# Key numbers of the chosen pairs in a PEER router: an exclusive-or with ranked numbers and a minimum in place of compare, multiply and add

## The chip, the cores and the metric

The kernel runs on one core of one Trainium2 chip. The metric is the device time of one execution in microseconds (us), lower is better. The engines named below are PE (matrix products; PEld is its weight load), DVE (the vector engine), ACT (the scalar engine), POOL (GpSimd, which here mostly issues row gathers) and SP (whose queue issues the large weight loads).

## The reference, cut to what matters

One layer of a hybrid backbone over 640 tokens (128 context tokens, 512 latent ones), that is five tiles of 128 tokens. After the attention half of the layer comes PEER, an expert retrieval. Per token and head, a query is scored against two sets of 128 keys, the best 16 of each side are kept, the 16 by 16 sums are ranked again, and the best 16 pairs name the experts:

```python
s_half, i_half = lax.top_k(s, PEER_TOPK)
cand = s_half[:, :, 0, :, None] + s_half[:, :, 1, None, :]
cand_idx = i_half[:, :, 0, :, None] * N_KEYS + i_half[:, :, 1, None, :]
top_s, top_pos = lax.top_k(cand.reshape(t, PEER_HEADS, PEER_TOPK * PEER_TOPK), PEER_TOPK)
experts = jnp.take_along_axis(cand_idx.reshape(...), top_pos, axis=-1)
gates = jax.nn.softmax(top_s, axis=-1)
# per token: y = sum over its 128 experts of gate * gelu(u[expert] . x) * v[expert]
```

There are 8 heads, so 128 experts for each token.

## The kernel before, in words

**Tiles.** Tile 0 is the context; tiles 1 to 4 are the latent tokens. The router takes the tiles in the order 0, 1, 3, 4, 2. Tiles 0, 1 and 2 are "gathered": POOL fetches, for each of the 128 experts of a token, one row of `expert_u` for 128 tokens at once (128 rows of 4 KB) into one of eight slots, DVE multiplies and sums it with the tokens (one "dot", line 1341), and the slot is free again for POOL. Rows of `expert_v` are gathered likewise and added with weights (line 1585). Tiles 3 and 4 are "dense": PE multiplies them with all 16384 experts, streamed by SP as 128 blocks of 512 KB from `expert_uT` (line 795) and later 128 blocks of `expert_v` (line 858).

**The router.** `rank_keys` (lines 1527 to 1534) finds the best 16 keys of four half-heads at a time, `route(e, part)` has six parts: part 0 builds the candidate sums and the key numbers as floats (line 1426, a cast of 128x256) and finds the best eight, parts 1 and 2 find the places and the next eight, part 3 splits a place into two digits (lines 1444 to 1452) and looks up the first side's key numbers, part 4 looks up the second side's, part 5 makes expert numbers and gates. The look-up is `key_numbers(side)`, lines 1416, 1418 and 1420: compare each of the 128 digits with 0 to 15 (a cube of 8x16x16 = 2048 columns), multiply by the 16 key numbers, and add over the last axis. Each pass waits for the one before it.

**Order on DVE.** Everything on DVE is in program order. The stages: attention of the context; the merge and norm of tile 0; `choose(0)`, which is `rank_keys` and `route` of tile 0; four groups of eight dots of tile 0; `convolve(1)` (lines 1285 to 1300), for which ACT waits; three more groups; attention of the latent tokens with dots between its units; merges and norms of tiles 1 to 4 with value rows of tile 0 between them; `choose(1)` with value rows between its pieces; then `rank_keys` and `route` of tiles 3, 4 and 2, with a group of eight dots of tile 1 after most pieces (after the pieces named in `DOTS_AFTER`: parts 1, 3 and 5 of each tile's route among them); ten groups of dots of tile 2; then `gates()`, 32 steps of building one-hot rows (line 1627) and products with the gates, which wait in their turn for PE's last block of `expert_uT`; the rest of the dots; and the late values. PE's placement of gates (line 845) follows DVE's one-hot rows, and its stream over `expert_v` (line 858) follows the last product.

**Order on POOL.** POOL's gathers of tile 0 wait for the end of route(0) (line 596 and on), those of tile 1 for the end of route(1) and for all value rows of tile 0. POOL fetches in fours: after four dots have freed four slots it copies four row numbers (line 518) and issues four gathers (line 523).

Of the kernel before, what the change touches and what calls it, by code (L numbers as in the profile page):

```python
# [19 lines left out]
ALU = mybir.AluOpType  # L20
ACT = mybir.ActivationFunctionType
AX = mybir.AxisListType.X
F32 = mybir.dt.float32
U32 = mybir.dt.uint32

P = 128
# [13 lines left out]
PEER_HEADS, TOPK, NKEYS = 8, 16, 128  # L40
HK = PEER_HEADS * TOPK
CAND = TOPK * TOPK
KEPT = CAND // 2
GROUP = 8
GROUPS = HK // GROUP
SCALE = HD ** -0.5
# [98 lines left out]
def backbone(nc, x_prompt, x_sample, xT, ck_T, cache_v, c_T, w_ada, b_ada, w_in, convw_T, w_branch,  # L145
# [10 lines left out]
    with ExitStack() as ctx:  # L156
        def sem(name):
            return ctx.enter_context(nc.semaphore(name))
# [52 lines left out]
        EQ = [at({0: 14336, 1: 28672}.get(e, 45056), PEER_HEADS, CAND) for e in range(TILES)]  # L211
        LATE = {e: at(o, 4, HALF) for e, o in ((1, 26624), (3, 35840), (4, 37888), (2, 39936))}

        VR = [UR] + [[at(26624 + 1024 * i, D) for i in range(GROUP)]] * (TILES - 1)
        U2B = [at(47104, D), at(44032, D), at(47104, D)]
# [8 lines left out]
        def keep(*shape):  # L224
            v = at(small[0], *shape)
            small[0] += int(np.prod(shape))
            return v
# [3 lines left out]
        IDXS = keep(2 * PEER_HEADS * TOPK).bitcast(U32)  # L231
# [3 lines left out]
        IDXF = keep(2 * PEER_HEADS * TOPK)  # L235
# [7 lines left out]
        MODT, CONVW, MASK, IOTA = keep(16, 2), keep(4, 3), keep(3, COL_BAND), keep(NKEYS)  # L243
        CT2, SIL, SEL = keep(KD, 2), keep(KD, 2), keep(2)
        NMAX, RSUM, RINV = keep(3, 4), keep(3, 4), keep(3, 4)
        STAT, MV, RSTD = keep(12), keep(2), keep(2)
        SMAX, TOPS, GSUM = keep(HK), keep(PEER_HEADS, TOPK), keep(PEER_HEADS)
        POS, PA, AF, BF = SW[:, 0, :].bitcast(U32), SW[:, 1, :].bitcast(U32), SW[:, 2, :], SW[:, 3, :]
        assert small[0] <= 53184, small[0]

# [66 lines left out]
        dgelu_out, spread_done, spread_out = sem("dgelu_out"), sem("spread_done"), sem("spread_out")  # L317
        hot_i, hot_j = sem("hot_i"), sem("hot_j")
        gated, placed = sem("gated"), sem("placed")
        product = sem("product")  # L320
        zero_set, rank_done, rank_out = sem("zero_set"), sem("rank_done"), sem("rank_out")
        cols_ready, summed = sem("cols_ready"), sem("summed")

# [909 lines left out]
        def _(dve):  # L1233
# [66 lines left out]
                dve.tensor_tensor(Cy[:, :, own], Cy[:, :, own], ct, ALU.mult).then_inc(conv_step, 1)  # L1300

            dve.wait_ge(consts_in, 48)
            convolve(0)
            for g in range(5, 8):
                add_mods(g)
# [62 lines left out]
            def route(e, part):  # L1368

                base = PICKED[e] - PICKS_OF[e]  # L1370
                val = VAL.rearrange("p (h s k) -> p h s k", s=2, k=TOPK)
                idxf = IDXF.rearrange("p (h s k) -> p h s k", s=2, k=TOPK)
                cube = [P, PEER_HEADS, TOPK, TOPK]
                if part == 0:
                    dve.wait_ge(topk_step, 80 * (TURN[e] + 1))
                if part == 0 and e == 1:
                    dve.wait_ge(store_out[1], 48)
                if part == PARTS - 1 and e == 2:
                    dve.wait_ge(rank_done, 1)
                if part == 3 and e == 1:  # L1380
                    dve.wait_ge(store_out[0], 64)
                    dve.wait_ge(ut_done, TILES)
                if part == 3 and e == 3:
                    dve.wait_ge(ss_done, 4 * TILES)
                if part or e:
                    dve.wait_ge(pick_step, base + ROUTE_AT[part])
                step = [base + ROUTE_AT[part]]

                def done(ins):
                    step[0] += 1  # L1390
                    ins.then_inc(pick_step, 1)

                def settle():
                    dve.wait_ge(pick_step, step[0])

                cands = CANDS[e][:, :, 0:KEPT].rearrange("p h (a b) -> p h a b", b=TOPK)
                eq = EQ[e].rearrange("p h (a b) -> p h a b", b=TOPK)
                pos = POS.rearrange("p (h k) -> p h k", k=TOPK)
                smax = SMAX.rearrange("p (h k) -> p h k", k=TOPK)
                iota = IOTA[:, 0:TOPK].unsqueeze(1).unsqueeze(1).to_broadcast(cube)  # L1400
                digits = DIGITS[e] if e in DENSE else (AF, BF)
                gate = DGATE[e] if e in DENSE else GATE[e % 2]

                def best(lo):

                    for h in range(PEER_HEADS):
                        done(dve.max(TOPS[:, h, lo:lo + 8], CANDS[e][:, h, 0:KEPT]))

                def places(lo):
                    for h in range(PEER_HEADS):  # L1410
                        done(dve.max_index(pos[:, h, lo:lo + 8], TOPS[:, h, lo:lo + 8], CANDS[e][:, h, 0:KEPT]))

                def key_numbers(side):

                    digit = digits[side].rearrange("p (h k) -> p h k", k=TOPK)
                    done(dve.tensor_tensor(eq, digit.unsqueeze(3).to_broadcast(cube), iota, ALU.is_equal))
                    settle()
                    done(dve.tensor_tensor(eq, eq, idxf[:, :, side, :].unsqueeze(2).to_broadcast(cube), ALU.mult))
                    settle()
                    done(dve.tensor_reduce(digit, eq, AX, ALU.add))  # L1420

                if part == 0:
                    half = [P, PEER_HEADS, TOPK // 2, TOPK]
                    done(dve.tensor_tensor(cands, val[:, :, 0, 0:TOPK // 2].unsqueeze(3).to_broadcast(half),
                                           val[:, :, 1, :].unsqueeze(2).to_broadcast(half), ALU.add))
                    done(dve.tensor_copy(IDXF, IDXS))
                    settle()
                    done(dve.tensor_tensor(CANDS[e][:, :, KEPT - 8:KEPT], val[:, :, 0, TOPK // 2:TOPK],
                                           val[:, :, 1, 0:1].to_broadcast([P, PEER_HEADS, 8]), ALU.add))
                    settle()  # L1430
                    best(0)
                elif part == 1:
                    places(0)
                    settle()
                    for h in range(PEER_HEADS):
                        done(dve.match_replace(CANDS[e][:, h, 0:KEPT], TOPS[:, h, 0:8], CANDS[e][:, h, 0:KEPT], LOWEST))
                elif part == 2:
                    best(8)
                    settle()
                    places(8)  # L1440
                    done(dve.tensor_tensor(smax, TOPS, TOPS[:, :, 0:1].to_broadcast([P, PEER_HEADS, TOPK]), ALU.subtract))
                elif part == 3:
                    place = TOPS.rearrange("p h k -> p (h k)")
                    done(dve.tensor_scalar(PA, POS, 4, None, ALU.logical_shift_right))
                    done(dve.tensor_copy(place, POS))
                    done(dve.tensor_scalar(POS, POS, TOPK - 1, None, ALU.bitwise_and))
                    settle()
                    done(dve.tensor_copy(digits[0], PA))
                    done(dve.tensor_copy(digits[1], POS))
                    settle()  # L1450
                    done(dve.scalar_tensor_tensor(digits[0], place, float(8 + 8 - KEPT), digits[0], ALU.add, ALU.max))
                    done(dve.scalar_tensor_tensor(digits[1], place, float(KEPT - 8), digits[1], ALU.is_lt, ALU.mult))
                    settle()
                    key_numbers(0)
                elif part == 4:
                    key_numbers(1)
                else:
                    if e == 1:
                        done(dve.scalar_tensor_tensor(PICKS, AF, float(NKEYS), BF, ALU.mult, ALU.add))
                        settle()  # L1460
                        done(dve.tensor_copy(EID[1], PICKS))
                    elif e not in DENSE:
                        done(dve.scalar_tensor_tensor(EID[e % 2], AF, float(NKEYS), BF, ALU.mult, ALU.add))
                    dve.wait_ge(gexp_done, TURN[e] + 1)
                    done(dve.tensor_reduce(GSUM, smax, AX, ALU.add))
                    settle()
                    done(dve.reciprocal(GSUM, GSUM))
                    settle()
                    done(dve.tensor_tensor(gate.rearrange("p (h k) -> p h k", k=TOPK), smax,
                                           GSUM.unsqueeze(2).to_broadcast([P, PEER_HEADS, TOPK]), ALU.mult))  # L1470
                assert step[0] == base + (ROUTE_AT[part + 1] if part < PARTS - 1 else PICKS_OF[e]), (part, step[0] - base)

# [228 lines left out]
FIN = 10  # L1701
SUB_AT = 3 + 5 * PEER_HEADS + 1

ROUTE_AT = (0, 3 + PEER_HEADS, 3 + 3 * PEER_HEADS, SUB_AT, SUB_AT + 10, SUB_AT + 13, SUB_AT + 17)
PARTS = len(ROUTE_AT) - 1
PICKS_OF = [ROUTE_AT[-1] + {1: 1, 3: -1, 4: -1}.get(e, 0) for e in range(TILES)]
PICKED = {e: sum(PICKS_OF[a] for a in ORDER[:n + 1]) for n, e in enumerate(ORDER)}
# [73 lines left out]
```

## Time and profile before

| | before |
|---|---|
| median of 3 runs | 2054.41 us (2049.19 to 2054.97) |
| the profiled execution, its own time | 2050.8 us |
| its span, first to last instruction | 2049.0 us |
| PE busy | 1851.6 us (90%) |
| DVE busy | 1342.7 us (66%) |
| POOL busy | 960.1 us (47%) |
| DMA, mean | 327 GB/s |

The profile is one execution. A busy share is an average over stages with different limits, so it is read stage by stage below. In a timeline row the first number is the start from the beginning of the span and the second the duration, both in us; the bracket at the end is the idle time of the engine before it and what ended that. The span lies 1.8 us below the execution's own time.

### The profile page before, as it was taken

The numbers are of one execution on the slowest core, as the hardware profiler recorded it, in microseconds if no ns is written. First come the engines' busy times: TensorE is split into PE (matmuls) and PEld (weight loads), VectorE is DVE, ScalarE is ACT, GpSimd is POOL, SyncE is SP. The second block draws the span as 40 slices with busy tenths as digits, with TensorE's granted clock in tenths as the row PEclk, the third lists the DMA queues.
The fourth block names the chain that finished last, engine by engine and source line by source line (L and its number), as shares of the span: only waits on it lengthen the run. The fifth ranks groups of instructions, "written<-read, shape, count | busy, mean of one in ns | idle before, by whom it ended". The sixth has DMA issues, their size and how long they took to land.

```text
span 2049.0 us, 22920 instructions
## 1 busy us (share of the span) xinstructions
PE 1851.6 (90%) x8148; PEld 1195.8 (58%) x8148; DVE 1342.7 (66%) x2645; ACT 284.8 (14%) x660; POOL 960.1 (47%) x1028
## 2 busy tenths in 40 slices
PE   5978799989899969998999999995789899979996
PEld 2756744457544436997888888883554333324442
DVE  1121476689758868999989886668986513335677
ACT  0120010036400001111110010004650000000000
POOL 1020027567645522325536556677766646535540
PEclk8999899989999989999999999997999999989998
DMA  8995638888899997548998999998889989999995
GB/s 360 366 378 204 256 139 301 279 318 298 287 349 329 318 365 257 187 165 303 338 373 327 394 341 405 406 396 278 273 296 410 399 326 409 410 409 398 409 409 217
DMA packets 166676, 670.19 MB, mean 327 GB/s; under 512 B 19340, under 2 KB 19468, under 8 KB 160940
## 3 DMA queue, kind: packets, MB, share of 16 engines
q0 software_dynamic: 112480, 410.79, 54.4%
q1 hardware_dynamic: 50352, 245.91, 30.7%
q10 hardware_dynamic: 3744, 12.14, 1.6%
q8 instruction: 65, 1.06, 0.2%
q14 instruction: 35, 0.29, 0.0%
HBM read 659.27 MB, written 7.39 MB: 325 GB/s over the span
## 4 chain that ended last, share of the span: by engine, by line
DMA 25%; PE 23%; DVE 20%; issue 16%; POOL 15%; POOLq 0%; ACTq 0%; ACT 0%; DVEq 0%
PE psum L858 13%; POOL arena L523 13%; DMA arena<-in_expert_u_dram,arena 12%; DMA arena<-in_expert_v_dram,arena 9%; DVE arena L1341 4%; DVE psum L1585 3%; PE psum L907 2%; PE psum L659 2%; PE psum L823 2%; DVE arena L1531 2%; DMA arena<-in_w_ada_dram 2%; POOL arena L518 2%; DVE arena L1527 1%; DVE arena L1627 1%; PE psum L634 1%
## 5 line engine op out<-in xcount | busy, mean ns | idle before, releaser
L1341 DVE CUSTOM_DVE_ANT_0 arena<-arena 128x1024 f32<-128x1024 f32 x384 | 462.3, 1225 | 197.7 <-DMA arena<-in_expert_u_dram,arena 190.9
L523 POOL DMA_INDIRECT arena<-in_expert_u_dram,arena x384 | 471.1, 1227 | 168.6 <-issue 98.9
L1585 DVE SCALAR_TENSOR_TENSOR psum<-arena,psum 128x1024 f32<-128x1024 f32 x254 | 327.2, 1288 | 221.2 <-DMA arena<-in_expert_v_dram,arena 204.8
L523 POOL DMA_INDIRECT arena<-in_expert_v_dram,arena x384 | 390.0, 1016 | 169.7 <-issue 102.5
L795 PE MATMUL psum<-arena 128*128 128x256 f32 x2048 | 444.5, 380 | 5.9 <-DMA arena<-in_expert_uT_dram 5.9
L858 PE MATMUL psum<-arena 128*128 128x512 f32 x1024 | 445.4, 595 | 2.0 <-DMA arena<-in_expert_v_dram 2.0
L795 PEld LDWEIGHTS psum<-arena 128*128 128x128 f32 x2048 | 389.7, 191 | 59.5 <-issue 6.3
L858 PEld LDWEIGHTS psum<-arena 128*128 128x128 f32 x1024 | 193.7, 191 | 257.0 <-issue 255.6
L518 POOL COPY arena<-arena 128x4 uint32 (+1 forms) x192 | 60.6, 316 | 425.1 <-DVE psum L1585 180.6
L938 PE MATMUL psum<-arena 128*128 128x128 f32 x1280 | 152.4, 280 | 4.8 <-issue 3.1
L938 PEld LDWEIGHTS psum<-arena 128*128 128x128 f32 x1280 | 149.0, 196 | 7.0 <-issue 6.3
L671 PE MATMUL psum<-arena 128*128 128x512 f32 x320 | 139.6, 598 | 2.7 <-ACT arena L1016 2.7
L671 PEld LDWEIGHTS psum<-arena 128*128 128x128 f32 x320 | 61.2, 192 | 80.2 <-issue 76.7
L845 PE MATMUL psum<-arena 128*128 128x128 f32 x512 | 67.2, 287 | 38.0 <-DVE arena L1627 37.9
L823 PE MATMUL psum<-arena 128*32 128x512 f32 x512 | 69.6, 666 | 26.6 <-DMA arena<-in_expert_v_dram,arena 26.5
L845 PEld LDWEIGHTS psum<-arena 128*128 128x128 f32 x512 | 62.0, 198 | 53.7 <-issue 53.7
L1172 ACT ACTIVATE arena<-psum 128x512 f32<-128x512 f32 x64 | 38.1, 597 | 383.3 <-PE psum L795 310.7
L907 PE MATMUL psum<-arena 128*128 128x512 f32 x160 | 74.1, 625 | 16.5 <-DVE arena L1484 9.4
L1180 ACT ACTIVATE arena<-arena 128x128 f32<-128x128 f32 x256 | 78.2, 388 | 59.6 <-DVE arena L1627 57.2
L872 PE MATMUL psum<-arena 128*128 128x128 f32 (+1 forms) x256 | 73.5, 442 | 3.0 <-ACT arena L1112 2.6
L1627 DVE TENSOR_TENSOR arena<-arena 128x1024 f32<-128x1024 f32 x64 | 75.5, 1220 | 0.3 <-DVE arena L1346 0.3
L875 PE MATMUL psum<-arena 128*128 128x128 f32 (+1 forms) x256 | 72.3, 436 | 1.7 <-DMA arena<-in_w_in_dram 1.7
(175 smaller groups left out, 1472.7 us busy)
## 6 DMA issues: line engine op xcount, KB each, us to landing
arena<-in_expert_uT_dram SPq DMA_DIRECT2D x128, 512.0 KB
arena<-in_expert_v_dram SPq DMA_DIRECT2D x128, 512.0 KB
arena<-in_w_in_dram SPq DMA_DIRECT2D x16, 2048.0 KB, 11.4
arena<-in_w_ada_dram SPq DMA_DIRECT2D x12, 2048.0 KB, 8.8
arena<-in_w_query_dram SPq DMA_DIRECT2D x8, 2048.0 KB, 17.0
arena<-in_w_in_dram SPq DMA_DIRECT2D x16, 512.0 KB, 6.3
arena<-in_w_o_dram SPq DMA_DIRECT2D x4, 2048.0 KB
arena<-in_expert_u_dram,arena POOLq DMA_INDIRECT x384
```

Of the source, the lines that this page charges most:

```text
L518: pool.tensor_copy(NUM[side][:, own], source).then_inc(num_ready, 1)
L523: pool.indirect_dma_start(slots[b], None, table[0], bass.IndirectOffsetOnAxis(ap=NUM[side][:, b:b + 1], axis=0)).then_inc(land, 16)
L671: mm = pe.matmul(bank(i % 2), w[:, k, c * P:(c + 1) * P], UT[:, k, CTX:NT], start=k == 0, stop=k == KD - 1)
L795: mm = pe.matmul(b[:, i * DTOK:(i + 1) * DTOK], RINGS[n % RING][:, k * P:(k + 1) * P], UT[:, k, NT - DTOK:NT], start=k == 0, stop=k == KD - 1)
L823: mm = pe.matmul(bank(6 + hf)[QUAD * j:QUAD * (j + 1), :], COLUMNS[:, i + j // 2, first:first + QUAD], UR[b0 + j][:, hf * HALF:(hf + 1) * ...
L845: mm = pe.matmul(bank(2 * (i % 2) + t // 4)[:, t % 4 * NKEYS:(t % 4 + 1) * NKEYS], HOT_J[i % 2][:, t, :], HOT_I[i % 2][:, t, :], start=Tru ...
L858: mm = pe.matmul(bank(2 + 2 * d + hf), own, RINGS[load % RING][:, hf * HALF:(hf + 1) * HALF], start=n == 0, stop=n == NKEYS - 1)
L907: mm = pe.matmul(bank(2 * (e % 2) + hf), MT[s][:, k, loc], w[:, k, :], start=k == 0, stop=k == KD - 1)
L938: mm = pe.matmul(bank(i % 2)[:, c * P:(c + 1) * P], w[:, k, c * P:(c + 1) * P], UT[:, k, e * P:(e + 1) * P], start=k == 0, stop=k == KD - 1)
L1341: dve.tensor_tensor_reduce(UR[b], UR[b], U2B[e], 1.0, 0.0, ALU.mult, ALU.add, DOT[:, b:b + 1]).then_inc(u_free, 1)
L1585: dve.scalar_tensor_tensor(ys, row, weight, ys, ALU.mult, ALU.add).then_inc(v_free, 1)
L1627: dve.tensor_tensor(dst[i % 2], keys.to_broadcast(full), IOTA.unsqueeze(1).to_broadcast(full), ALU.is_equal).then_inc(done, 1)
```

## The change

The cast of the key numbers to floats becomes a bitwise or with the ranks 0 to 15 times 256, so that each of the 16 numbers of a side carries its rank above its eight low bits. The wanted digits are kept times 256 as integers. One exclusive-or of the cube then gives the plain key number where the ranks agree and something of at least 256 where they don't, and the minimum over the last axis is the key number. The ranks are made once, at the start, by one small instruction on DVE with a semaphore of its own. The pieces of the router keep their order; the counts of the route's semaphore (`ROUTE_AT`) drop accordingly.

```diff
+        RANKS = keep(TOPK).bitcast(U32)
+        NUMBERED = IDXF.bitcast(U32)
...
             dve.wait_ge(consts_in, 48)
+            dve.tensor_scalar(RANKS, IOTA[:, 0:TOPK], float(NEXT), None, ALU.mult).then_inc(ranks_set, 1)
             convolve(0)
...
                 if part == 0:
+                    dve.wait_ge(ranks_set, 1)
                     dve.wait_ge(topk_step, 80 * (TURN[e] + 1))
...
                 def key_numbers(side):
 
                     digit = digits[side].rearrange("p (h k) -> p h k", k=TOPK)
-                    done(dve.tensor_tensor(eq, digit.unsqueeze(3).to_broadcast(cube), iota, ALU.is_equal))
+                    wanted = (PA, POS)[side].rearrange("p (h k) -> p h k", k=TOPK)
+                    done(dve.tensor_tensor(found, wanted.unsqueeze(3).to_broadcast(cube),
+                                           numbered[:, :, side, :].unsqueeze(2).to_broadcast(cube), ALU.bitwise_xor))
                     settle()
-                    done(dve.tensor_tensor(eq, eq, idxf[:, :, side, :].unsqueeze(2).to_broadcast(cube), ALU.mult))
-                    settle()
-                    done(dve.tensor_reduce(digit, eq, AX, ALU.add))
+                    done(dve.tensor_reduce(digit, found, AX, ALU.min))
...
-                    done(dve.tensor_copy(IDXF, IDXS))
+                    done(dve.tensor_tensor(NUMBERED.rearrange("p (m k) -> p m k", k=TOPK),
+                                           IDXS.rearrange("p (m k) -> p m k", k=TOPK),
+                                           RANKS.unsqueeze(1).to_broadcast([P, 2 * PEER_HEADS, TOPK]), ALU.bitwise_or))
...
-                    done(dve.tensor_scalar(PA, POS, 4, None, ALU.logical_shift_right))
+                    done(dve.tensor_scalar(PA, POS, 4, 8, ALU.logical_shift_right, ALU.logical_shift_left))
                     done(dve.tensor_copy(place, POS))
-                    done(dve.tensor_scalar(POS, POS, TOPK - 1, None, ALU.bitwise_and))
+                    done(dve.tensor_scalar(POS, POS, TOPK - 1, 8, ALU.bitwise_and, ALU.logical_shift_left))
                     settle()
                     done(dve.tensor_copy(digits[0], PA))
                     done(dve.tensor_copy(digits[1], POS))
+                    done(dve.tensor_scalar(place, place, float(NEXT), None, ALU.mult))
                     settle()
-                    done(dve.scalar_tensor_tensor(digits[0], place, float(8 + 8 - KEPT), digits[0], ALU.add, ALU.max))
-                    done(dve.scalar_tensor_tensor(digits[1], place, float(KEPT - 8), digits[1], ALU.is_lt, ALU.mult))
+                    done(dve.scalar_tensor_tensor(PA, place, float(NEXT * (8 + 8 - KEPT)), digits[0], ALU.add, ALU.max))
+                    done(dve.scalar_tensor_tensor(POS, place, float(NEXT * (KEPT - 8)), digits[1], ALU.is_lt, ALU.mult))
...
-ROUTE_AT = (0, 3 + PEER_HEADS, 3 + 3 * PEER_HEADS, SUB_AT, SUB_AT + 10, SUB_AT + 13, SUB_AT + 17)
+ROUTE_AT = (0, 3 + PEER_HEADS, 3 + 3 * PEER_HEADS, SUB_AT, SUB_AT + 10, SUB_AT + 12, SUB_AT + 16)
```

## Rows read from the trace of the kernel before

**Rows 1.** The page's chain that ended last, shares by engine and by line.
```profile
DMA 25%; PE 23%; DVE 20%; issue 16%; POOL 15%; POOLq 0%; ACTq 0%; ACT 0%; DVEq 0%
```

**Rows 2.** Stages: busy us per engine (count), granted clock, DMA share, GB/s.
```profile
763.00:900.00 137.00, 133.53 (x993) 117.00 (x994) 128.33 (x297) 19.82 (x32) 32.82 (x41) 0.99 0.55 192
900.00:1060.00 160.00, 151.97 (x808) 135.89 (x808) 149.64 (x514) 22.76 (x34) 76.89 (x76) 0.97 0.88 327
1060.00:1200.00 140.00, 140.00 (x652) 123.21 (x651) 125.38 (x358) 18.46 (x29) 72.93 (x66) 1.00 0.94 357
1200.00:1300.00 100.00, 100.00 (x465) 88.00 (x464) 63.53 (x104) 8.75 (x16) 62.53 (x59) 1.00 1.00 391
```

**Rows 3.** DVE's groups by line and shape, all stages: busy us, mean ns.
```profile
L1418 DVE TENSOR_TENSOR arena<-arena 128x2048 f32<-128x2048 f32 x10 | 22.9, 2292 | 0.3
L1420 DVE TENSOR_REDUCE arena<-arena 128x128 f32<-128x2048 f32 x10 | 22.9, 2286 | 0.3
L1318 DVE SCALAR_TENSOR_TENSOR arena<-psum,arena 128x256 f32<-128x256 f32 x32 | 13.5, 422 | 0.5 <-DVE arena L1346 0.3
L1426 DVE CAST arena<-arena 128x256 f32<-128x256 uint32 x5 | 1.4, 287 | 0.0
L1444 DVE TENSOR_SCALAR arena<-arena 128x128 uint32<-128x128 uint32 x5 | 1.1, 226 | 0.2
```

**Rows 4.** Timeline of POOL: the first transfer behind tile 0's route.
```profile
291.15 0.56 POOL L596 DMA_DIRECT2D arena<-u_d  x1 [143.81 <-DVE arena L1469]
```

**Rows 5.** Timeline, start of the latent attention: ACT, PE and DVE.
```profile
378.46 1.08 ACT L1016 ACTIVATE arena<-psum 128x512 f32<-128x512 f32 x2 [15.16 <-DVE arena L1300]
```
```profile
379.11 41.45 PE L671 MATMUL psum<-arena 128*128 128x512 f32 x92 [2.71 <-ACT arena L1016]
```
```profile
428.73 1.19 PE L723 MATMUL psum<-arena 64*128 64x256 f32 x2 [4.63 <-DVE arena L1318]
```

**Rows 6.** Timeline of POOL: the first fetch for tile 1's dots.
```profile
899.41 0.18 POOL L518 COPY arena<-arena 128x4 uint32 x1 [24.98 <-DVE psum L1585]
```

**Rows 7.** Timeline of DVE: ends (L1346) and starts (L1341) of groups of tile 1's dots.
```profile
1058.29 0.17 DVE L1346 COPY arena<-arena 128x8 f32<-128x8 f32 x1
...
1071.06 1.22 DVE L1341 CUSTOM_DVE_ANT_0 arena<-arena 128x1024 f32<-128x1024 f32 x1
...
1080.34 0.17 DVE L1346 COPY arena<-arena 128x8 f32<-128x8 f32 x1
...
1088.81 1.22 DVE L1341 CUSTOM_DVE_ANT_0 arena<-arena 128x1024 f32<-128x1024 f32 x1
...
1101.67 0.17 DVE L1346 COPY arena<-arena 128x8 f32<-128x8 f32 x1
...
1112.47 1.20 DVE L1341 CUSTOM_DVE_ANT_0 arena<-arena 128x1024 f32<-128x1024 f32 x1
...
1121.74 0.17 DVE L1346 COPY arena<-arena 128x8 f32<-128x8 f32 x1
```

**Rows 8.** Timeline of POOL beside line 1416's and 1418's passes on DVE.
```profile
1081.42 2.75 POOL L523 DMA_INDIRECT arena<-in_expert_u_dram,arena  x1 [0.30 <-issue]
1084.48 2.02 POOL L523 DMA_INDIRECT arena<-in_expert_u_dram,arena  x1 [0.30 <-issue]
...
1087.49 0.97 POOL L523 DMA_INDIRECT arena<-in_expert_u_dram,arena  x1 [0.80 <-POOL arena L518]
```

**Rows 9.** Timeline of DVE: ends of groups of eight dots, then the one-hot rows.
```profile
1325.30 0.17 DVE L1346 COPY arena<-arena 128x8 f32 x1
...
1375.23 0.17 DVE L1346 COPY arena<-arena 128x8 f32 x1
...
1402.68 0.17 DVE L1346 COPY arena<-arena 128x8 f32 x1
1403.13 4.63 DVE L1627 TENSOR_TENSOR arena<-arena 128x1024 f32<-128x1024 f32 x4 [0.28 <-DVE arena L1346]
```

**Rows 10.** PE's line 795, the products with `expert_uT`: durations and first and last start.
```profile
L795 PE MATMUL psum<-arena x2048: 379/379/765, 933.9 to 1384.2; 128*128 128x256 f32 x187
```

More of the change, by code:

```diff
@@ L43 @@
 KEPT = CAND // 2
+NEXT = 256
 GROUP = 8
@@ L319, in backbone @@
         gated, placed = sem("gated"), sem("placed")
-        product = sem("product")
+        product, ranks_set = sem("product"), sem("ranks_set")
         zero_set, rank_done, rank_out = sem("zero_set"), sem("rank_done"), sem("rank_out")
@@ L1371, in route @@
                 val = VAL.rearrange("p (h s k) -> p h s k", s=2, k=TOPK)
-                idxf = IDXF.rearrange("p (h s k) -> p h s k", s=2, k=TOPK)
+                numbered = NUMBERED.rearrange("p (h s k) -> p h s k", s=2, k=TOPK)
                 cube = [P, PEER_HEADS, TOPK, TOPK]
                 if part == 0:
+                    dve.wait_ge(ranks_set, 1)
                     dve.wait_ge(topk_step, 80 * (TURN[e] + 1))
@@ L1396, in route @@
                 cands = CANDS[e][:, :, 0:KEPT].rearrange("p h (a b) -> p h a b", b=TOPK)
-                eq = EQ[e].rearrange("p h (a b) -> p h a b", b=TOPK)
+                found = EQ[e].bitcast(U32).rearrange("p h (a b) -> p h a b", b=TOPK)
                 pos = POS.rearrange("p (h k) -> p h k", k=TOPK)
                 smax = SMAX.rearrange("p (h k) -> p h k", k=TOPK)
-                iota = IOTA[:, 0:TOPK].unsqueeze(1).unsqueeze(1).to_broadcast(cube)
                 digits = DIGITS[e] if e in DENSE else (AF, BF)
```

## The prediction, as it was put on record

> **What bounds the kernel now.** I read the chain that ended last first. It belongs to nobody: DMA, PE, DVE and POOL hold 15 to 25% each [rows 1]. So the question is stage by stage: where do the passes of `key_numbers` lie, and what ends last behind them? There are ten of each kind, 2.29 us each [rows 3], two of each per tile.
>
> Tile 0's route is bare: POOL has idled 143.81 us when its last instruction releases the gathers [rows 4]. Tile 1's route is in a stage where DVE is busy 128.3 of 137 us and DMA only 0.55; the routes of tiles 3, 4 and 2 lie between about 930 and 1210 us, where DVE is busy 149.6 of 160 and 125.4 of 140 us; from 1200 on DVE drops to 63.5 of 100 and DMA is at 1.00 [rows 2]. PE looks like the bound there, but its products with `expert_uT` have their last start at 1384.2 [rows 10], while the one-hot rows that the next stage needs begin at 1403.13, right behind the last dots at 1402.68 [rows 9]. They may begin once PE's stream is over (1384.2 and one product of 0.38), so DVE and the gathers are late by 1403.1 - 1384.6 = 18.5 us, and that is the most that anything after PE's own start at 933.9 can give. What follows (placement, products, the stream over `expert_v`, the last values) is the same work from there, and shifts.
>
> **The change part by part.** *The removed pass.* Two passes of 2.29 us per route are gone [rows 3]: -4.58 us, if the exclusive-or costs what the compare and the product cost and the minimum what the sum cost. The trace shows no exclusive-or and no reduction of integers. Nearest rows: a two-tensor pass of the same cube, 2292 ns, and the same sum, 2286; for integers, a shift of 128 uint32 in 226 ns and a cast of 256 in 287 [rows 3], that is twice the columns for 61 ns more, so integers aren't read slowly. The rows of the cube are the nearest in size and shape, so I take 2.29 for both; the bad end is twice that for both, the good end 2.29, since even the reduction with one input takes that.
>
> *Added work.* The scaling of `place` is 128 columns of one input: 0.23 by line 1444, perhaps less as it overlaps its neighbours; I take 0.23, between 0.1 and that. The bitwise or is a two-tensor operation of 256 columns: 422 ns at line 1318 against the cast's 287 [rows 3], +0.13; between 0 and 0.2. The second operation in the two shifts adds no column: nothing, at most 0.1 each. So a route is 4.58 - 0.36 = 4.22 us shorter, and five 21.1 us: the ceiling. *The ranks* are 16 columns, once, in the first stage; below the 0.23 of 128 columns, I take nothing, at worst it is all on the path. The wait on `ranks_set` has long been met when the first route asks; no wait is added that is open, so nothing queues behind one. The transfers are the same, and none is moved past a queue.
>
> *Tile 0.* Route(0) ends 4.22 us earlier, and POOL starts its gathers so much earlier. Two things run from there to the start of the latent attention. ACT waits 15.16 us for the convolution on DVE, and PE loses 2.71 us through it [rows 5]; with the convolution 4.2 us earlier all 2.71 come back and no more, since PE's own products bound then. And DVE is the later of the two, for PE waits 4.63 us for the first window [rows 5]; DVE's dots move by up to 4.2. The attention then moves by 2.7 to 4.2; the gathers in between meet 2 MB weight loads that move by their own waits. I take the middle, 3.5. Attention, merges, norms and PE's stream itself shift with it.
>
> *Tile 1.* POOL has idled 24.98 us when the last value row of tile 0 lets it fetch for tile 1 [rows 6], and that row is behind route(1) on a DVE that is nearly full: -4.22.
>
> *Tiles 3, 4 and 2.* Here lumps of router work lie between groups of eight dots, and a saving counts only if the rows for the next group have landed by then. There are two kinds of gap. The group after part 3 needs no wait: tile 4's begins at 1071.06 and its eight end at 1080.34, back to back [rows 7]. The gap ahead of it, from 1058.29, is 12.8 us and goes to 10.7. A gap of 10.8 without a wait stands in the same rows, 1101.67 to 1112.47, with its eight done at 1121.74. So I count 2.29 - 0.23 = 2.06 us in all three tiles, and the 2.29 of tile 3's second side, behind which the norm of tile 0 lengthens the gap. The or costs 0.13 in each. Together 6.18 + 2.29 - 0.39 = 8.1 us. The group after parts 4 and 5 of tiles 4 and 2 is different: 8.5 us lie between 1080.34 and 1088.81, and its eight take until 1101.67, 12.9 us in place of 9.3 [rows 7]: they wait for rows. There a shorter gap by itself becomes a longer wait. What helps is POOL: beside the two passes its gathers take 2.75 and 2.02 us to issue, right behind them 0.97 [rows 8]. With one pass, one of the two is short again, and requests go out 2.02 - 0.97 = 1.05 us earlier. Two such places give 2.1 of their 4.6 us.
>
> The Trainium skill, "GPSIMD Engine Reference", section Specifications, says that GpSimd's SBUF interfaces are shared with VectorE and contended by DVE instructions with two SBUF inputs. The trace agrees (2.75 and 2.02 beside the passes, 0.97 behind). By that page the exclusive-or, with two inputs too, still holds POOL for its one pass, as I counted it.
>
> *Given back.* Sum of the stage: 4.22 + 8.1 + 2.1 = 14.4 us, below the 18.5. But the gathers run slow while PE streams and fast once its loads have ended: 24 dots in 1375.23 - 1325.30 = 49.9 us, 2.08 each, and then 16 in 27.45 us, 1.72 each [rows 9]. A chain that ends 14.4 us earlier does this part of its gathers at the slow rate: 14.4 x (1 - 1.72/2.08) = 2.5 us back. Left: 11.9.
>
> *Sum.* 3.5 + 11.9 = 15.4 us. The profiled execution took 2050.8 us, of which 2049.0 are its span; it would be 2035.4. That execution is 3.6 us below the median of the runs shown, so for a median I take the same difference from 2054.4: 2039.0 us.
>
> **The rivals.** *Gathers bound the stage from 930 on.* The DMA share is 0.88 to 0.94 there, and the group after the short gap does wait [rows 7]; against it, 327 and 357 GB/s are below the 391 reached later [rows 2]. Then tiles 3, 4 and 2 give nothing, and what is left is 3.5 + 4.22 - 0.7 (the same 17% of it) = 7.0 us: 2047.4. *All of it arrives.* Every second is on the path and the gathers follow: 2054.4 - 21.1 = 2033.3. It needs the attention to move by 4.2 and POOL's relief to cover both waited gaps; the slow tail speaks against it. *Integer passes are slower.* Place: the cube passes alone. A route's look-ups then cost 2(x + r) + 0.36 in place of 6 x 2.29 = 13.74 us, with x for the exclusive-or and r for the minimum. Nothing is gained at x + r = 6.7, against 4.6 by the rows, and it is slower by over 0.3% (1.24 us a route) from 7.3. At double length for both, 9.16, it is five times +4.9 = 24.7 us, 2079.1. For it: no row shows either operation at this size. Against it: the 226 and 287 ns of the integers [rows 3]. If only the exclusive-or doubles, x + r = 6.9, five times +0.4: 2056. That the change doesn't do what it says (a third pass left, or ranks and numbers overlapping) is hard to see: numbers are below 128 and ranks start at 256; it would show as wrong experts, not as time.
>
> **How the numbers follow.** Forecast 0.58; gathers bound 0.22; all of it 0.09; exclusive-or alone slow 0.06; both integer passes slow 0.05. I count 0.3% (6.2 us) as what a measurement can tell from no change. Faster: the first three, but of the gather case, whose 7.0 us are only just above that, 0.16: 0.58 + 0.16 + 0.09 = 0.83. Same: its other 0.06 and the 0.06 of the exclusive-or alone, 0.12. Slower: 0.05. The range reaches from the full gain (2033.3, and 2.3 for the spread of runs) to the gather case and the small end of its sum (attention 2.7, spread 2): 2031 to 2050.
>
> **What would show it.** DVE's cube passes 20 in place of 30, 2.29 us each, busy time of DVE lower by about 21 us. POOL's first transfer behind route(0) at 286.9 in place of 291.2, PE's idle of 2.71 gone; POOL's first fetch for tile 1 near 891.7; the one-hot rows near 1387.7, still some 6 us behind PE's last product at about 1381; the last span from there unchanged at 646 us. Wrong would be: a pass other than 2.29 us; waits for `expert_u` in the groups after part 3; one-hot rows that start where they did.

## The result, and the profile after

| | before | after |
|---|---|---|
| median | 2054.97 us (19 runs) | 2038.9 us (19 runs) |
| ratio, 95% interval | 1 | 0.9928 [0.9910, 0.9947]: 14.8 us less (10.9 to 18.5); the medians differ by 16.1 |
| span of the profiled execution | 2049.0 us | 2035.9 us |

The kernel is 0.7% faster, close to what was forecast (15.4 us). DVE's groups in the changed kernel, in the form of [rows 3]:

```profile
L1421 DVE TENSOR_TENSOR arena<-arena 128x2048 uint32<-128x2048 uint32 x10 | 22.9, 2291 | 0.8 <-DVE arena L1350 0.6
L1424 DVE TENSOR_REDUCE arena<-arena 128x128 f32<-128x2048 uint32 x10 | 22.9, 2286 | 0.3
L1430 DVE TENSOR_TENSOR arena<-arena 128x256 uint32<-128x256 uint32 x5 | 2.1, 419 | 0.0
L1456 DVE TENSOR_SCALAR arena<-arena 128x128 f32<-128x128 f32 x5 | 1.1, 219 | 0.0
L1306 DVE TENSOR_SCALAR arena<-arena 128x16 uint32<-128x16 f32 x1 | 0.2, 155 | 0.0
```

Twenty passes stand in place of thirty. The exclusive-or (line 1421) and the minimum (line 1424) of integers take to within a nanosecond what the product and the sum took; the or is 419 ns, the scaling 219.

The stages answer to [rows 2]:

```profile
763.00:900.00 137.00, 134.64 (x1079) 123.64 (x1078) 129.67 (x378) 21.09 (x34) 40.42 (x50) 1.00 0.60 212
900.00:1060.00 160.00, 154.89 (x779) 137.99 (x779) 146.53 (x460) 24.52 (x35) 74.69 (x72) 0.98 0.89 336
1060.00:1200.00 140.00, 140.00 (x653) 123.55 (x652) 115.89 (x335) 15.49 (x25) 78.61 (x73) 1.00 0.94 356
1200.00:1300.00 100.00, 100.00 (x466) 88.24 (x465) 59.56 (x102) 9.34 (x17) 62.54 (x58) 1.00 1.02 402
```

DVE's busy time between 900 and 1200 us fell from 275.0 to 262.4. Two profiles can't be subtracted, though. The first instruction of tile 0's route starts at 262.5 us in before and here at

```profile
255.05 1.23 DVE L1428 TENSOR_TENSOR arena<-arena 128x1024 f32<-128x1024 f32 x1
```

so 7.4 of the 13.1 us between the two spans were there before any changed work of the router. Executions differ that much among themselves: the 19 of the changed kernel lie between 2027.9 and 2053.0. I therefore cut each profile at the same four marks and compare kernels by stretch, over the runs of this study whose look-ups in that stretch are of the same length. The marks are starts in timelines: the first candidate sum of tile 0; the first window of the latent attention; POOL's first fetch for tile 1; the first one-hot rows; the last stretch runs to the end of the span. The last three of these marks are in the changed kernel

```profile
419.27 0.42 DVE L1322 SCALAR_TENSOR_TENSOR arena<-psum,arena 128x256 f32<-128x256 f32 x1 [0.28 <-DVE arena L1350]
```
```profile
883.80 0.18 POOL L521 COPY arena<-arena 128x4 uint32 x1 [20.46 <-DVE psum L1592]
```
```profile
1389.21 3.50 DVE L1634 TENSOR_TENSOR arena<-arena 128x1024 f32<-128x1024 f32 x3 [0.28 <-DVE arena L1350]
```

| kernel | 1: to the latent attention | 2: to the first fetch | 3: to the one-hot rows | 4: to the end |
|---|---|---|---|---|
| before | 165.7 | 471.2 | 503.7 | 645.9 |
| before, again | 167.6 | 474.9 | 501.5 | 647.5 |
| after | 164.3 | 464.5 | 505.4 | 646.7 |
| after, again | 162.6 | 471.0 | 501.8 | 645.4 |
| new in tile 0 alone | 164.7 | 478.2 | 508.2 | 647.4 |
| new in tile 1 alone | 169.4 | 469.3 | 505.5 | 648.1 |
| new in tiles 3, 4, 2 alone | 166.9 | 475.8 | 494.3 | 651.0 |
| exclusive-or twice | 168.7 | 471.2 | 506.4 | 648.0 |
| minimum twice | 170.1 | 479.8 | 502.8 | 648.0 |
| no look-up in tiles 3, 4 | 163.2 | 465.4 | 498.1 | 646.7 |
| 18 passes more in 3, 4, 2 | 164.0 | 474.3 | 520.0 | 652.1 |
| 8 passes more in tile 1 | 163.2 | 492.3 | 501.2 | 644.9 |
| 8 passes more in tile 0 | 185.7 | 468.0 | 497.8 | 645.3 |
| tree of 16-bit minima | 162.9 | 464.0 | 500.9 | 647.7 |

All in us. A single entry of stretches 2 and 3 is good to some 4 us, one of stretch 1 to 2. So a difference of two means of stretch 3 is known to some 3 us. Stretch 4, in which nothing differs, lies between 644.9 and 652.1.

Two shorter distances are free of this spread. Both start at a route's first instruction, its candidate sum. In before these are

```profile
262.47 1.23 DVE L1424 TENSOR_TENSOR arena<-arena 128x1024 f32<-128x1024 f32 x1
```
```profile
854.17 1.22 DVE L1424 TENSOR_TENSOR arena<-arena 128x1024 f32<-128x1024 f32 x1
```

for tiles 0 and 1, and in the changed kernel the row at 255.05 above and

```profile
842.95 1.22 DVE L1428 TENSOR_TENSOR arena<-arena 128x1024 f32<-128x1024 f32 x1
```

From tile 0's sum to POOL's first transfer behind the route it is 28.68 us in before (291.15, [rows 4]) and 24.29 in the changed kernel (279.34, shown further below): 4.39 less. From tile 1's sum to POOL's first fetch for tile 1 it is 45.24 us in before (899.41, [rows 6]) and 40.85 in the changed kernel (883.80): 4.39 less. Over all profiles with the same look-up in that tile each of the four numbers repeats to within 0.1 us. That is the price of the change for one route, measured.

### The profile page after: what moved, and what is told of

Same layout as the page of the kernel before. It is cut to its first block, busy times and chain, and to the rows that moved or that the text cites. A ratio compares the mean times of both kernels' runs of the same rounds, so it can differ in the third digit from the quotient of the medians.

```text
span 2035.9 us, 22917 instructions
## 1 busy us (share of the span) xinstructions
PE 1840.2 (90%) x8148; PEld 1192.9 (59%) x8148; DVE 1317.0 (65%) x2641; ACT 284.9 (14%) x660; POOL 960.4 (47%) x1028
## 4 chain that ended last, share of the span: by engine, by line
DMA 31%; POOL 18%; issue 18%; DVE 18%; PE 13%; POOLq 1%; ACT 0%; ACTq 0%; DVEq 0%
POOL arena L526 16%; DMA arena<-in_expert_v_dram,arena 15%; DMA arena<-in_expert_u_dram,arena 13%; PE psum L861 5%; DVE arena L1345 4%; DVE psum L1592 3%; PE psum L910 2%; POOL arena L521 2%; DVE arena L1538 2%; PE psum L826 2%; DVE arena L1534 1%; PE psum L662 1%; DMA arena<-in_w_ada_dram 1%; DMA arena<-in_w_in_dram 1%; DVE arena L1541 1%
## 5 line engine op out<-in xcount | busy, mean ns | idle before, releaser
L1345 DVE CUSTOM_DVE_ANT_0 arena<-arena 128x1024 f32<-128x1024 f32 x384 | 462.1, 1225 | 219.8 <-DMA arena<-in_expert_u_dram,arena 218.1
L526 POOL DMA_INDIRECT arena<-in_expert_u_dram,arena x384 | 476.4, 1241 | 168.6 <-issue 92.3
L526 POOL DMA_INDIRECT arena<-in_expert_v_dram,arena x384 | 383.5, 999 | 169.4 <-issue 91.6
L941 PE MATMUL psum<-arena 128*128 128x128 f32 x1280 | 148.6, 278 | 1.6 <-ACT arena L1126 1.2
L848 PE MATMUL psum<-arena 128*128 128x128 f32 x512 | 66.6, 287 | 36.6 <-DVE arena L1634 35.6
L910 PE MATMUL psum<-arena 128*128 128x512 f32 x160 | 73.6, 621 | 22.6 <-DVE arena L1491 15.5
```

What stands on the lines that cost most here:

```text
L526: pool.indirect_dma_start(slots[b], None, table[0], bass.IndirectOffsetOnAxis(ap=NUM[side][:, b:b + 1], axis=0)).then_inc(land, 16)
L848: mm = pe.matmul(bank(2 * (i % 2) + t // 4)[:, t % 4 * NKEYS:(t % 4 + 1) * NKEYS], HOT_J[i % 2][:, t, :], HOT_I[i % 2][:, t, :], start=Tru ...
L910: mm = pe.matmul(bank(2 * (e % 2) + hf), MT[s][:, k, loc], w[:, k, :], start=k == 0, stop=k == KD - 1)
L941: mm = pe.matmul(bank(i % 2)[:, c * P:(c + 1) * P], w[:, k, c * P:(c + 1) * P], UT[:, k, e * P:(e + 1) * P], start=k == 0, stop=k == KD - 1)
L1345: dve.tensor_tensor_reduce(UR[b], UR[b], U2B[e], 1.0, 0.0, ALU.mult, ALU.add, DOT[:, b:b + 1]).then_inc(u_free, 1)
```

## The experiments

All are compared with before in the same session. Before against itself read 0.9983 [0.9966, 1.0000] in such a session, so a difference of 0.2% between two of these ratios, or of one of them from 1, says little.

### One place at a time

**Tile 0.** The old `route` stands for tiles 1, 3, 4 and 2.

```diff
+NUMBERS_NEW = (0,)
...
+                    if e not in NUMBERS_NEW:
+                        (the three passes of before)
```

> The new look-up in tile 0's route alone; tiles 1, 3, 4 and 2 keep compare, multiply and add. Theory of the prediction: route(0) is 4.2 us shorter and the attention starts 3.5 us earlier (2.7 to 4.2), so about -3.5 us in all, 0.998 of before; in the trace the stretch from the first candidate sum of tile 0 (262.5 in before) to the first window of the latent attention (428.2) is 165.7 - 3.5 = 162.2 us. Rival, that the gathers of tile 0 and the weight loads beside them set the start: the stretch stays within 1.5 us of 165.7. The stretch from POOL's first fetch for tile 1 to the one-hot rows stays at that of before (503.7 us) by both.

Measured: 0.9978 [0.9955, 1.0001], 4.5 us less. Stretch 1 is 164.7. The value expected was made from before's 165.7, which proved the lowest of its kind: the four profiles with old look-ups in tile 0 and nothing repeated have 165.7, 167.6, 169.4 and 166.9, mean 167.4, and the six with new ones (after twice, this one, and those altered in other tiles) 164.3, 162.6, 164.7, 163.2, 164.0 and 163.2, mean 163.7. That is 3.7 us less, with some 0.8 of uncertainty, against 3.5 forecast. The rival (within 1.5 us of before) falls by these means; the ratio alone can't be told from before's own 0.9983.

**Tile 1.**

> The new look-up in tile 1's route alone. Theory of the prediction: -4.2 us at POOL's first fetch for tile 1, of which 17% are given back in the tail of the gathers: -3.5 us in all, 0.998 of before; in the trace the stretch from the first window of the latent attention to that fetch is 471.2 - 4.2 = 467.0 us. Rival, that value rows or the norms set it: 471 us as before. The stretch from there to the one-hot rows 503.7 + 0.7 by both.

Measured: 0.9979 [0.9960, 0.9998], 4.3 us less; stretch 2 is 469.3. Means of stretch 2: 475.0 with the old look-up (471.2, 474.9, 478.2, 475.8), 468.8 with the new one (464.5, 471.0, 469.3, 465.4, 474.3, 468.0). 6.3 us less, with some 2 of uncertainty; 4.22 were forecast. The distance from tile 1's candidate sum to the fetch gives 4.39, so all of the route's saving arrives at the fetch; what goes beyond it lies ahead of the route, where the change in tile 1 has no part, and is spread. The rival, that value rows or the norms set the fetch, falls by that distance.

**Tiles 3, 4 and 2.**

> The new look-up in the routes of tiles 3, 4 and 2 alone. Theory of the prediction: 8.1 + 2.1 = 10.2 us of the 12.7 taken out, less 17%: -8.5 us in all, 0.996 of before; in the trace the stretch from POOL's first fetch for tile 1 to the one-hot rows is 503.7 - 8.5 = 495.2 us. Rival, that the gathers bound this stage: the stretch stays at 503 to 505 us, as it did in the changed kernel's own profile (505.4), DVE's waits for rows of expert_u in tile 1's dots grow by what the routes lose, and the time is that of before within 2 us.

Measured: 0.9965 [0.9943, 0.9988], 7.2 us less, with stretch 3 at 494.3. The rival of gathers that bound the whole stage had 2 us at most here, which lies just outside the interval, and 7.0 us for the whole change, which lies well outside its 10.9 to 18.5. But 494.3 is the lowest of its kind: the four with new look-ups there and nothing else in stretch 3 have 505.4, 501.8, 494.3 and 497.8, mean 499.8, the old ones 503.7, 501.5, 508.2 and 505.5, mean 504.7. That is 4.9 us less, with some 3 of uncertainty, where 7.7 were forecast (10.2 less the 2.5 given back). The means suggest that the forecast was high here and don't prove it; the point-by-point section looks at the gaps one by one.

The three ratios take 0.22, 0.21 and 0.35% off, 0.78 together, against 0.72 of the whole; each is known to 0.2 only.

### Is it the pass, and nothing else?

```diff
                     done(dve.tensor_tensor(found, wanted..., numbered..., ALU.bitwise_xor))
                     settle()
+                    dve.tensor_tensor(found, wanted..., numbered..., ALU.bitwise_xor).then_inc(repeated, 1)
+                    dve.wait_ge(repeated, repeats[0])
```

> The changed kernel with the exclusive-or run twice in every look-up, so that DVE has three passes of 2.29 us again, two of them with two inputs. Theory: the gain lies in the pass and in nothing else of the change, so the time is that of before plus the 0.36 us of added small work per route: +1.8 us at most, 1.000 to 1.001. Rival, that the gain measured (16 us between medians) is more than the passes give and has another source (place of the code, the counts of the semaphores, other waits): it stays below before by 5 us or more, 0.9975 or less.

Measured: 1.0013 [0.9990, 1.0036]. With the pass put back the gain is gone; the change's small operations and semaphores bring nothing of their own. Tile 0's route takes 28.96 us here, 0.28 more than in before: that is what the small added work costs, where I had 0.36.

**What POOL feels.** Here the minimum is run twice, which has one input.

> The changed kernel with the minimum run twice in every look-up: DVE has three passes of 2.29 us as in before, but only one of them has two inputs. Theory (POOL's gather requests are held beside passes with two inputs): the first gathers of the group after part 3 take 2.75 and then 0.97 us to issue in place of 2.75 and 2.02, and the two groups that wait for rows come up to 1.05 us earlier each; the time is 1 to 2 us below that of the kernel with the exclusive-or twice, 0.999 to 1.001 of before. Rival, that POOL is held by any pass of DVE: its requests look as in before, 2.75 and 2.02.

Measured: 1.0003 [0.9981, 1.0025], which can't be told from the exclusive-or twice. The trace can tell. POOL's gathers behind tile 4's group after part 3, first with the exclusive-or twice (passes from 1076.38 to 1081.00), then with the minimum twice (the exclusive-or from 1090.27 to 1092.56, minima behind it):

```profile
1077.10 2.40 POOL L527 DMA_INDIRECT arena<-in_expert_u_dram,arena  x1 [0.30 <-issue]
1079.80 2.02 POOL L527 DMA_INDIRECT arena<-in_expert_u_dram,arena  x1 [0.30 <-issue]
```
```profile
1090.98 2.40 POOL L527 DMA_INDIRECT arena<-in_expert_u_dram,arena  x1 [0.31 <-issue]
1093.69 0.94 POOL L527 DMA_INDIRECT arena<-in_expert_u_dram,arena  x1 [0.30 <-issue]
```

and in the changed kernel, the answer to [rows 8]:

```profile
1063.36 2.40 POOL L526 DMA_INDIRECT arena<-in_expert_u_dram,arena  x1 [0.30 <-issue]
1066.07 0.94 POOL L526 DMA_INDIRECT arena<-in_expert_u_dram,arena  x1 [0.30 <-issue]
```

A pass with one input of the same 2.29 us holds no gather, one with two does. In the profile with the minimum twice, five gathers start beside an exclusive-or and take 2.40 to 2.96 us, and nine beside a minimum, which take 0.94 to 0.96. The 1.05 us that I counted is there (2.02 - 0.94 = 1.08). "POOL is held by any pass" falls. What the 1.08 us are worth in time wasn't resolved.

### What a microsecond of DVE is worth in the late stage

```diff
+                    for _ in range(3 if e in (3, 4, 2) else 0):
+                        (the exclusive-or again, as above)
```

> The changed kernel with three more exclusive-ors in each look-up of tiles 3, 4 and 2: 18 passes of 2.29 us, 41 us more on DVE between POOL's first fetch for tile 1 and the one-hot rows. Theory (DVE is late in this stage, up to the 17% that the slow tail of the gathers takes): that stretch is 34 to 41 us longer than the changed kernel's, which I put at 495 us, so 529 to 536, and the time is 1.009 to 1.013 of before. Rival, that gathers bound the stage and DVE has room there: at least half of the 41 us disappears in DVE's waits for rows of expert_u (102 us in the changed kernel's profile), the stretch is below 520 us and the time below 1.003.

Measured: 1.0050 [1.0031, 1.0070], stretch 3 at 520.0. Against the changed kernel's 0.9928 that is 1.22%, 25 us for 41, 0.6 of each; by the stretch (499.8 to 520.0) it is 20 us, 0.5 of each. Both lie between theory and rival, and neither holds as stated.

> The changed kernel without the look-ups of tiles 3 and 4: a copy of 128 columns stands in place of the four exclusive-ors and the four minima, 18.3 - 0.9 = 17.4 us less on DVE. What is left out: the key numbers of the dense tiles, whose one-hot rows then hit other keys or none. Theory: the gap ahead of the group after part 3 falls from 10.7 to 6.3 us and the one after it from 6.3 to 2, below the 8 us at which groups already wait, so most becomes waiting; I expect a third, 6 us, less 17%: the stretch from the first fetch for tile 1 to the one-hot rows is 490 us (495 - 5), and the time 2.5 to 5 us below the changed kernel, 0.990 to 0.9915 of before. Rival, that DVE bounds this stage throughout: all but 17% arrives, the stretch is 481 us and the time 0.986 of before, until PE's stream becomes the bound.

Measured: 0.9920 [0.9894, 0.9946], stretch 3 at 498.1. 17.4 us less on DVE bring 1.7 us, in the ratios (0.9928 to 0.9920) as in the stretch (499.8 to 498.1), with an interval of some 6 us either way. "DVE bounds throughout" (0.986) lies outside the interval; my third (0.990 to 0.9915) lies inside. So the gain per microsecond seems to fall with the load: 41 us more cost 20 to 25, the removed passes brought 5 to 7 of 12.7, the next 17 bring 1.7. Where the curve bends isn't shown by two points this uncertain. DVE's idle time for rows of `expert_u` over the whole kernel is 190.9 and 189.9 us in the two profiles of before, 218.1 and 201.9 in those of the changed kernel, 226.4 here.

### Tiles 1 and 0 with eight passes more

> The changed kernel with four more exclusive-ors in each look-up of tile 1's route: 8 passes, 18.3 us more on DVE ahead of POOL's first fetch for tile 1. It is the term of tile 1 and the part that the tail gives back, four times as large. Theory of the prediction: the fetch is 18.3 us later (the stretch from the first window of the latent attention to it 467 + 18 = 485 us), the stretch from it to the one-hot rows 17% of that shorter, 3.1 us (497), and the time 15.2 us above the changed kernel's: 1.000 of before. Rival, that the later stage has room (18 passes more in it cost 25 of 41 us, 0.6 of them): the time rises by 11 us or less, 0.998.

Measured: 1.0011 [0.9987, 1.0035], stretch 2 at 492.3, stretch 3 at 501.2. From the 0.9928 of the changed kernel this is 17 us for 18.3, from the 0.9909 that it had beside the same runs of before 21; the rival (11 us or less) is unlikely, and 15.2 and 18.3 can't be told apart. From tile 1's candidate sum to the fetch it is 59.48 us, 18.6 more than in the changed kernel; that stretch 2 grew by 23.5 is spread for the rest. Stretch 3 isn't 3 us shorter than the 499.8 of its kind, but it is known to 4 only.

> The changed kernel with four more exclusive-ors in each look-up of tile 0's route: 18.3 us more on DVE ahead of tile 0's gathers and of the convolution. Theory: the start of the latent attention moves by all of it, for DVE is the later of the two there and PE loses what the convolution loses: the stretch from tile 0's first candidate sum to the first window is 163.8 (mean of the five profiles with the new look-up in tile 0) + 18.3 = 182 us, all later stages unchanged, time 1.0017 of before. Rival, that part is covered by PE's projection and the weight loads (I counted 3.5 of 4.2 us): 0.83 of it arrives, the stretch is 179 us, the time 1.000.

Measured: 1.0031 [1.0014, 1.0047], stretch 1 at 185.7, that is 22.0 us more for 18.3. ACT's wait for the convolution shows where the rest is:

```profile
393.30 43.91 PE L675 MATMUL psum<-arena 128*128 128x512 f32 x96 [22.21 <-ACT arena L1020]
```

and in the changed kernel, the answer to [rows 5]:

```profile
369.13 23.44 PE L674 MATMUL psum<-arena 128*128 128x512 f32 x54 [0.25 <-ACT arena L1019]
```

PE's projection lost 22.21 us in place of 0.25, as much as stretch 1 grew. So nothing covers tile 0's route when it is lengthened. The route itself, up to POOL's first transfer, is 18.6 us longer (42.91 us in place of 24.29), 2.33 for each pass. Why these become 22.0 on the way through four groups of gathered dots wasn't tested.

### Once more, and a candidate

> The changed kernel once more, for a second profile of its stages and a second interval: 0.993 of before; by the means of the profiles so far 164 us from the first candidate sum to the first window, 467 to the first fetch for tile 1, 498 (between 494 and 505) to the one-hot rows, 647 to the end. If the third of these is 505 again, as in its first profile, the gain of tiles 3, 4 and 2 is smaller than the 8.5 us of the prediction.

> The kernel before once more, for a second profile of its stages: ratio 1.000; 168 us, 475, 505 and 647 in the four stretches by the means of the profiles whose look-ups are as long.

Measured: 0.9909 [0.9887, 0.9930] for the changed kernel, 18.7 us less (14.4 to 23.2), and 0.9983 for before. So the rival "all of it arrives" (21.1 us) lies outside the first interval but inside this one. The four stretches stand in the table; the third is 501.8, between the two values that the expectation weighed. DVE is busy 1322.4 us in the one and 1343.6 in the other, 21.2 less. Between the first two profiles it is 25.7, but there before holds one copy of 4.30 us (line 1346, else 0.17), and the changed kernel none; the second profiles hold one such long instruction each.

```diff
-                    done(dve.tensor_reduce(digit, found, AX, ALU.min))
+                    for n, width in enumerate((8, 4, 2)):
+                        v = levels[n]      # 16-bit values
+                        done(dve.tensor_tensor(levels[n + 1], v[:, :, :, 0:width], v[:, :, :, width:2 * width], ALU.min))
+                        settle()
+                    ...
```

> A candidate for a faster kernel: the changed kernel's exclusive-or on the low 16 bits of the numbers, written as 16-bit values, and the minimum as a tree of four two-input minima (1024, 512, 256 and 128 columns out) in place of one reduction. If 16-bit pairs run at twice the rate of the 32-bit ones (1.22, 0.69, 0.42 and 0.29 us for these sizes in before), the tree takes 0.7 + 0.4 + 0.3 + 0.2 = 1.6 us in place of 2.29, ten times, 7 us less on DVE and some 4 to 5 us less in all: 0.990 of before. If they run at the same rate, the tree takes 2.6 us and the time is 2 to 3 us above the changed kernel's, 0.994.

```profile
L1427 DVE TENSOR_TENSOR arena<-arena 128x2048 uint16<-128x2048 uint16 x10 | 22.9, 2292 | 0.8 <-DVE arena L1351 0.6
L1432 DVE TENSOR_TENSOR arena<-arena 128x1024 uint16<-128x1024 uint16 x10 | 6.9, 692 | 0.3
L1432 DVE TENSOR_TENSOR arena<-arena 128x512 uint16<-128x512 uint16 x10 | 4.3, 425 | 0.3
L1432 DVE TENSOR_TENSOR arena<-arena 128x256 uint16<-128x256 uint16 x10 | 2.9, 292 | 0.3
L1435 DVE TENSOR_TENSOR arena<-arena 128x128 f32<-128x128 uint16 x10 | 2.9, 293 | 0.3
```

The tree takes 1.70 us in place of 2.29, at twice the 32-bit rate as hoped (692 ns for 1024 columns against 1225). The time is 0.9929 [0.9911, 0.9947], where 0.990 was expected. It can't be told from the changed kernel's 0.9928, and a gain of 2 us couldn't be seen either. The route of tile 0 takes 23.35 us, 0.94 less. If the late stage gives as little as with no look-up in tiles 3 and 4, some 2 us from tiles 0 and 1 are all that is left; that is argued and not measured.

## Why the prediction was right, point by point

**The removed pass and the added work: right.** I had -4.58 + 0.36 = -4.22 us per route; the durations give -4.58 + 0.22 + 0.13 = -4.23, the two distances 4.39, and the second pair of profiles 21.2 us in all. The distance is larger since a pass takes 2.33 us with its semaphore and the added work only 0.28. The case of slow integers fell at once.

**Tile 0: right**, 3.7 against 3.5 us. PE's idle of 2.71 us went to 0.25; over the four profiles with old look-ups there it is 3.9 on average (2.7 to 5.8), over the six with new ones some 0.4 (1.5 at most). POOL's first transfer behind the route has idled 138.72 us in place of 143.81 [rows 4]:

```profile
279.34 0.56 POOL L599 DMA_DIRECT2D arena<-u_d  x1 [138.72 <-DVE arena L1476]
```

The clock times that I named (286.9 here, 891.7, 1387.7) were of little use, as a different execution had shifted by 7 us before the route began; I should have named stretches.

**Tile 1: right**, 4.39 us by the distance to the fetch, 6.3 by the stretch and 4.3 by the ratio, against 4.22.

**Tiles 3, 4 and 2: the mechanism right, one gap misjudged.** The distance from the end of one group of eight dots to the end of the next (line 1350's copies, line 1346's in before), in four profiles with old look-ups there and in four with new ones:

| the gap holds | old | new | mean | forecast |
|---|---|---|---|---|
| tile 3, parts 2, 3 | 22.3 22.5 23.5 22.6 | 23.6 23.1 21.6 21.3 | -0.3 | -2.06 |
| tile 3, parts 4, 5 | 21.6 22.5 21.6 21.6 | 19.3 19.3 19.4 21.1 | -2.1 | -2.29 |
| tile 4, parts 2, 3 | 22.0 22.0 22.1 22.0 | 19.9 19.9 19.9 19.9 | -2.1 | -2.06 |
| tile 4, parts 4, 5 | 21.3 21.7 21.0 21.3 | 21.7 21.8 20.1 22.9 | +0.3 | -1.05 |
| tile 2, parts 2, 3 | 22.3 22.1 22.1 22.2 | 19.9 20.0 20.7 20.0 | -2.0 | -2.06 |
| tile 2, parts 4, 5 | 23.6 22.0 23.6 22.2 | 21.9 21.8 20.2 21.0 | -1.6 | -1.05 |

(old: before twice, new in tile 0 alone, new in tile 1 alone; new: after twice, new in tiles 3, 4, 2 alone, 8 passes more in tile 0.) The two kinds of gap are as I had them, and four of the six terms are within 0.6 us. The first one isn't (-0.3, with 0.6 of uncertainty): the step that failed is "So I count 2.29 - 0.23 = 2.06 us in all three tiles". In the changed kernel tile 3's group after part 3 does wait, which the prediction had named as a sign of being wrong:

```profile
943.05 1.22 DVE L1345 CUSTOM_DVE_ANT_0 arena<-arena 128x1024 f32<-128x1024 f32 x1
...
949.27 1.23 DVE L1345 CUSTOM_DVE_ANT_0 arena<-arena 128x1024 f32<-128x1024 f32 x1 [0.41 <-DMA arena<-in_expert_u_dram,arena]
...
951.83 1.23 DVE L1345 CUSTOM_DVE_ANT_0 arena<-arena 128x1024 f32<-128x1024 f32 x1 [1.32 <-DMA arena<-in_expert_u_dram,arena]
...
954.40 1.22 DVE L1345 CUSTOM_DVE_ANT_0 arena<-arena 128x1024 f32<-128x1024 f32 x1 [1.34 <-DMA arena<-in_expert_u_dram,arena]
```

I had judged three places by the row of one. DVE waits 3.1, 2.6, 1.1 and 1.2 us for rows in this group in the four new profiles, and 0.0, 0.0, 0.8 and 0.0 in the four old ones. Why here and not in tile 4's or tile 2's stays open. That the group before had waited itself isn't the reason: tile 4's group before waits 5.8 us in the changed kernel, and the next one not at all. Nor is the loss constant. With 8 passes more in tile 1, a kernel that is new in tiles 3, 4 and 2 and stands in neither column, the same gap is 19.9 us without a wait. Over the whole run of fourteen gaps the means are 294.2 and 285.9 us, 8.3 less, where I had 10.2; this sum is known to some 3 us, so only the single gap is shown to be off.

**Given back: right in size; its cause is only argued.** The eleven gaps after those, in which every row is waited for, add to 180.2 us with the old look-ups (179.1, 180.2, 178.6, 182.9) and to 183.8 with the new (184.4, 183.8, 182.7, 184.1): 3.6 back, with 1 of uncertainty, against 2.5. The kernel with 18 passes more, which comes latest (it begins them at 1239.4), does them in 176.2, as it should if whoever comes early to PE's stream pays. But the one with 8 passes more in tile 1 comes late too (at 1230.9) and takes 184.8, so that rule doesn't explain all. The ends in the changed kernel, the answer to [rows 9]:

```profile
1359.36 0.17 DVE L1350 COPY arena<-arena 128x8 f32 x1
1372.89 0.17 DVE L1350 COPY arena<-arena 128x8 f32 x1
1388.77 0.17 DVE L1350 COPY arena<-arena 128x8 f32 x1
```

29.4 us for 16 dots where before has 27.45 (27.7 and 27.2 in the second profiles). What remains of the stage is 8.3 - 3.6 = 4.7 us, the 4.9 of stretch 3. And PE's stream wasn't the bound:

```profile
L798 PE MATMUL psum<-arena x2048: 378/380/767, 915.8 to 1365.8; 128*128 128x256 f32 x187
```

it ends 23.0 us ahead of the one-hot rows here (18.5 in before), 13.3 in the second profile, and never less than 9.3 in any profile of the table.

**The sum.** 3.7 + 6.3 + 4.9 = 14.9 us by stretches, 14.8 by the ratio, 15.4 forecast. That the median came within 0.1 us of the forecast is chance: the stretches add up only because tile 1's is 2 us above its term and that of tiles 3, 4 and 2 is 3 us below, and each interval is wider than that. What stays open: why tile 0's route costs more than its length when it is lengthened, why tile 3's group after part 3 waits, and what decides how much the last eleven gaps give back.

## What to carry to other kernels

A saving on an engine that alternates with gathered rows has to be priced gap by gap: it arrives in full where the next group's rows have landed (here 2.0 to 2.1 us in each of three gaps), and mostly not where they are waited for (-0.3, +0.3 and -1.6 us in the other three), and the rows of one such gap don't speak for another. Then ask what it arrives at: coming earlier into a stretch in which rows are waited for all the time gave 3.6 of 8.3 us back here. And where single executions differ by as much as the change brings, compare stretches between the same marks over several profiles, and put the marks as near to the changed work as they go: over 40 us the saving repeated to 0.1 us, over 500 it was lost in a spread of 4. A clock time of one profile proves nothing.

## What the runs showed of the hardware that I had not expected

- A pass of DVE with two inputs in SBUF holds POOL's gather beside it (2.40 and 2.02 us in place of 0.94), a reduction of the same 2.29 us doesn't.
- An exclusive-or of 16-bit values whose inputs are broadcast and read in steps of two takes 2292 ns for 2048 columns, as at 32 bits; a minimum of two 16-bit halves, read in steps of one, takes 692 ns for 1024, against 1225 at 32 bits.
- What a microsecond of DVE is worth in one and the same stage depends on its load: 0.5 to 0.6 us per us with 41 us more than in the changed kernel, 0.1 with 17 us less. The second is known to 0.4 only.
